# Two joints of a float32 encoder trunk rebuilt: halves of the last unit, raw residual turned, 1/rms applied late

## The reference

```python
def rms_norm(x, g):
    y = xf * lax.rsqrt(jnp.mean(xf * xf, axis=-1, keepdims=True) + NORM_EPS)
    return (y * g.astype(jnp.float32)).astype(x.dtype)
...
x = x + jnp.concatenate([oa, ob], axis=-1) @ w_out_e[i]          # first output projection
x = x + (silu(h @ w_gate) * (h @ w_up)) @ w_down                 # dense layer, h = rms_norm(x, ln_ffn_e)
h = rms_norm(x, ln_mix_o[j])
qc, kc, vc = jnp.split(h @ na_w_qkv[j], 3, axis=-1)              # neighbourhood attention
x = x + neighborhood_attention(qc, kc, vc, na_rpb[j]) @ na_w_out[j]
x = x + moe_swiglu(rms_norm(x, ln_ffn_o[j]), ...)                # top-2-of-8 experts
return rms_norm(x, ln_final)
```

## Time and profile before

| what | us |
| --- | --- |
| median of three runs | 1477.28 |
| lowest and highest of them | 1470.55, 1479.37 |
| the profiled execution, its own time | 1470.76 |
| its span | 1469.0 |
| PE, DVE, ACT busy in the span | 1432.2, 1116.0, 958.9 |

### The profile page before, as it was taken

One profiled execution on the slowest core, in us unless ns is written; L12 is line 12 of the kernel. 1 busy time (PEld: TensorE's weight loads), 2 busy tenths in 40 slices (PEclk: granted clock), 3 DMA queues, 4 the chain that ended last, 5 costly groups with the idle time before them and its releaser, 6 DMA issues.

```text
span 1469.0 us, 20948 instructions
## 1 busy us (share of the span) xinstructions
PE 1432.2 (97%) x7757; PEld 1224.7 (83%) x7757; DVE 1116.0 (76%) x843; ACT 958.9 (65%) x866; POOL 113.7 (8%) x99
## 2 busy tenths in 40 slices
PE   8989999999999999999999999999999999999996
PEld 7887999998987788888888888888888888888885
DVE  4574544456464698988888888898888888888886
ACT  6473443445354577777777777777777777777774
POOL 4340000000000110020001002002002000000100
PEclk9999999999999999999999999999999999999998
DMA  9422855554512499999999999999999999999992
GB/s 338 177 87 86 210 197 173 198 172 160 190 52 80 163 370 376 367 359 394 395 357 395 390 357 384 395 373 367 394 378 366 394 380 354 394 393 362 392 396 106
DMA packets 205850, 435.94 MB, mean 297 GB/s; under 512 B 8192, under 2 KB 53376, under 8 KB 205808
## 3 DMA queue, kind: packets, MB, share of 16 engines
q1 hardware_dynamic: 198176, 418.01, 78.2%
q0 software_dynamic: 3904, 14.42, 3.2%
q10 hardware_dynamic: 3728, 2.95, 1.0%
HBM read 428.02 MB, written 7.34 MB: 296 GB/s over the span
## 4 chain that ended last, share of the span: by engine, by line
PE 92%; DVE 5%; ACT 2%; issue 1%; DMA 0%; DVEq 0%; SPq 0%; ACTq 0%
PE banks L1274 29%; PE banks L1276 29%; PE banks L1275 29%; PE banks L1620 2%; PE banks L1467 1%; DVE w_lo L808 1%; DVE xn L821 1%; ACT arena L586 0%; PE banks L1586 0%; DVE arena L982 0%; PE banks L1289 0%; PE banks L1455 0%; PE banks L1396 0%; DMA xres<-in_x 0%; PE banks L1330 0%
## 5 line engine op out<-in xcount | busy, mean ns | idle before, releaser
L808 DVE TENSOR_TENSOR w_lo<-raw,w_hi 128x2048 fp32r<-128x2048 f32 (+1 forms) x396 | 904.1, 2291 | 221.3 <-ACT w_hi L453 220.4
L453 ACT CAST w_hi<-raw 128x2048 fp32r<-128x2048 f32 (+1 forms) x396 | 756.7, 1911 | 244.6 <-PE banks L1276 236.1
L1274 PE MATMUL banks<-w_hi,t_hi 128*128 128x512 f32 (+2 forms) x1088 | 416.4, 383 | 4.7 <-DVE w_lo L842 2.4
L1276 PE MATMUL banks<-w_lo,t_hi 128*128 128x512 f32 (+2 forms) x1088 | 410.9, 378 | 0.0
L1275 PE MATMUL banks<-w_hi,t_lo 128*128 128x512 f32 (+2 forms) x1088 | 410.5, 377 | 0.0
L1274 PEld LDWEIGHTS banks<-w_hi,t_hi 128*128 128x128 f32 x1088 | 205.6, 189 | 41.4 <-DVE w_lo L842 2.6
L1276 PEld LDWEIGHTS banks<-w_lo,t_hi 128*128 128x128 f32 x1088 | 205.5, 189 | 38.2
L1275 PEld LDWEIGHTS banks<-w_hi,t_lo 128*128 128x128 f32 x1088 | 205.7, 189 | 36.0 <-issue 0.2
L1274 PE MATMUL banks<-w_hi,h_hi 128*128 128x512 f32 x536 | 209.6, 391 | 0.7 <-DVE w_lo L808 0.7
L1276 PE MATMUL banks<-w_lo,h_hi 128*128 128x512 f32 x536 | 208.8, 390 | 0.0
L1275 PE MATMUL banks<-w_hi,h_lo 128*128 128x512 f32 x536 | 208.7, 389 | 0.0
(11 more groups left out here) (235 smaller groups left out, 937.1 us busy)
## 6 DMA issues: line engine op xcount, KB each, us to landing
raw<-in_moe_w_gate SPq DMA_DIRECT2D x112, 1024.0 KB, 7.8
raw<-in_moe_w_up SPq DMA_DIRECT2D x112, 1024.0 KB, 8.2
raw<-in_moe_w_down SPq DMA_DIRECT2D x112, 1024.0 KB, 8.1
raw<-in_na_w_qkv SPq DMA_DIRECT2D x12, 1024.0 KB, 5.1
raw<-in_ffn_w_gate SPq DMA_DIRECT2D x11, 1024.0 KB, 5.5
raw<-in_ffn_w_up SPq DMA_DIRECT2D x11, 1024.0 KB, 5.2
raw<-in_ffn_w_down SPq DMA_DIRECT2D x11, 1024.0 KB, 4.9
raw<-in_w_in_e SPq DMA_DIRECT2D x6, 1024.0 KB, 19.9
```

The source lines that it names most:

```text
L453: act.copy(w_hi[:, u.part, 0:n], raw[:, u.raw, 0:n]).then_inc(hi_done, 1)
L808: dve.tensor_tensor(w_lo[:, u.part, 0:n], raw[:, u.raw, 0:n], w_hi[:, u.part, 0:n].bitcast(F32), ALU.subtract).then_inc(lo_done, 1)
L1274: pe.matmul(out, a_hi, b_hi, start=start, stop=False)
L1276: return pe.matmul(out, a_hi, b_lo, start=False, stop=stop)
```

## The change

- The last unit of the first output projection and of the dense layer is computed by column halves (`rows_by_half`): all matmuls of columns 0 to 511 first, then those of columns 512 to 1023; the first half signals `half_mm`. DVE adds the residual in four 128 x 512 pieces (`residual_by_half`), the first two after the first half.
- `turn_x` turns the raw residual, half by half, in place of xn. `keep_busy` is gone at both joints. `turned_hi` and `turned_lo` split with the gain per partition (`gain_t` now holds four gains, the DMA of it is four times as large), 1/rms is computed afterwards (`row_stats`, `row_factors`).
- 1/rms is applied later: in the dense layer to the gate (a new DVE multiplication with `r_row` into `act_g`, silu then works in place) and to the output, as the factor of `residual_by_half`; in the neighbourhood layer to values (two ACT instructions with scale in place of one copy), to keys (a DVE multiplication into `k_tmp_c`, in xn, from which ACT and DVE split), and to the scores through `rq`. Two more `spread_rows`: after the first gate unit, and after the second unit of the neighbourhood projection.
- The gains of the last two norms are loaded at the start on POOL's queue; the loads of two others are gone, and with them two DMAs from ACT's queue.
- The second output projection and its joint stay as they were.

Lines with only "..." mark what is left out.

```diff
+BY_HALF = (U_OUT0,)
...
+        k_tmp_c = xn[:].rearrange("p t (i a s) -> p (t i) a s", i=2, a=2)
...
+            def turned_hi(q, n, bank):
+                for i in range(4):
+                    act.wait_ge(t_mm, 4 * q + i + 1)
+                    for k in (2 * i, 2 * i + 1):
+                        last = act.activation(t_hi[:, k, :], banks[:, bank + i, (k % 2) * SEQ:(k % 2 + 1) * SEQ],
+                                              ACT.Copy, scale=gain_t[:, n, k:k + 1])
+                    last.then_inc(t_hi_done, 1)
+            def row_stats(n):
+                for t in range(T):
+                    act.activation(xn[:, t, :], xres[:, t, :], ACT.Square,
+                                   accum_out=sums_sq[:, t:t + 1]).then_inc(ss_done, 1)
+                act.wait_ge(ms_done, 2 * n + 2)
+                act.activation(std[:], mean_sq[:], ACT.Sqrt).then_inc(std_done, 2)
...
-            norm_stats(1, ACT.Silu)
-            split_t_hi(2)
+            warm(ACT.Sqrt)
+            turned_hi(2, 1, 0)
+            row_stats(1)
+            warm(ACT.Silu)
             hi(Unit(U_FFN + 2))
-            act.wait_ge(xn_ready, 4)
-            act.dma_start(gains[:, 1, :], over_partitions(ln_ffn_o, D)).then_inc(gain_in[3], 16)
+            act.wait_ge(row_mm, 2)
+            act.copy(r_row[:], banks[:, 3, 0:SEQ]).then_inc(row_out, 1)
...
-                act.wait_ge(used, u.count())
-                act.activation(act_g[:], banks[:, 4 + 2 * jj, :], ACT.Silu).then_inc(silu_done, 1)
+                act.wait_ge(gate_scaled, j + 1)
+                act.activation(act_g[:], act_g[:], ACT.Silu).then_inc(silu_done, 1)
...
                 elif i < 8:
-                    last = act.copy(vc[:, :, 256 * (i - 4):256 * (i - 4) + 256], src)
+                    act.wait_ge(rstd_done, 6)
+                    for t in range(T):
+                        last = act.activation(vc[:, t, 256 * (i - 4):256 * (i - 4) + 256], src[:, t, :], ACT.Copy,
+                                              scale=rstd[:, t:t + 1])
                 else:
-                    last = act.copy(kc_t[0][:, 2 * (i - 8):2 * (i - 8) + 2, :], src)
+                    act.wait_ge(k_scaled, 2 + i - 7)
+                    last = act.copy(kc_t[0][:, 2 * (i - 8):2 * (i - 8) + 2, :], k_tmp_c[:, i - 8])
...
+            def turned_lo(q, n, bank):
+                for i in range(4):
+                    dve.wait_ge(t_hi_done, 4 * q + i + 1)
+                    for k in (2 * i, 2 * i + 1):
+                        last = dve.scalar_tensor_tensor(
+                            out=t_lo[:, k, :], in0=banks[:, bank + i, (k % 2) * SEQ:(k % 2 + 1) * SEQ],
+                            scalar=gain_t[:, n, k:k + 1], in1=t_hi[:, k, :].bitcast(F32),
+                            op0=ALU.mult, op1=ALU.subtract)
+                    last.then_inc(t_lo_done, 1)
+            def row_factors(n):
+                dve.wait_ge(ss_done, 2 * n + 2)
+                dve.tensor_scalar(mean_sq[:], sums_sq[:], 1.0 / D, EPS, ALU.mult, ALU.add).then_inc(ms_done, 2)
+                dve.wait_ge(std_done, 2 * n + 2)
+                dve.reciprocal(rstd[:], std[:]).then_inc(rstd_done, 2)
+                dve.wait_ge(rstd_done, 2 * n + 2)
+                dve.tensor_scalar(rq[:], rstd[:], HD ** -0.5, None, ALU.mult)
+                for t in range(T):
+                    last = dve.tensor_scalar(diag[:, t, :], ident, rstd[:, t:t + 1], None, ALU.mult)
+                last.then_inc(diag_ready, 1)
...
-                            in0=scores[:, cut].rearrange("p (r c) -> p r c", r=4), scalar=HD ** -0.5,
+                            in0=scores[:, cut].rearrange("p (r c) -> p r c", r=4), scalar=rq[:, t:t + 1],
...
+            def residual_by_half(n, bank, u, factor=None):
+                for c in range(2):
+                    if c == 0:
+                        dve.wait_ge(half_mm, n)
+                    else:
+                        dve.wait_ge(used, u + 1)
+                    for t in range(T):
+                        cols = xres[:, t, c * HALF:(c + 1) * HALF]
+                        out_half = banks[:, bank + 2 * t + c, :]
+                        if factor is None:
+                            dve.tensor_tensor(cols, cols, out_half, ALU.add).then_inc(x_tile, 1)
+                        else:
+                            dve.scalar_tensor_tensor(out=cols, in0=out_half, scalar=factor[:, t:t + 1], in1=cols,
+                                                     op0=ALU.mult, op1=ALU.add).then_inc(x_tile, 1)
...
-            residual(4, U_OUT0 + 3)
-            dve.wait_ge(x_tile, 2)
-            norm_apply(1, 1)
-            split_t_lo(2)
+            residual_by_half(1, 4, U_OUT0 + 3)
+            turned_lo(2, 1, 0)
+            row_factors(1)
             lo(Unit(U_FFN + 2))
-            def ffn_dve(j, jj):
+            def ffn_dve(u_g, u_u, j, jj):
+                dve.wait_ge(used, u_g.count())
+                both = lambda w: w.rearrange("p (k s) -> p k s", k=2)
+                dve.tensor_tensor(both(act_g), both(banks[:, 4 + 2 * jj, :]),
+                                  r_row[:].unsqueeze(1).broadcast_to([P, 2, SEQ]), ALU.mult).then_inc(gate_scaled, 1)
                 dve.wait_ge(silu_done, j + 1)
+                dve.wait_ge(used, u_u.count())
                 dve.tensor_tensor(hid[:], act_g[:], banks[:, 5 + 2 * jj, :], ALU.mult).then_inc(hid_done, 1)
...
                 elif i >= 8:
-                    c = slice(2 * (i - 8), 2 * (i - 8) + 2)
-                    rest(kc_t[1][:, c, :], kc_t[0][:, c, :], 4 + i % 4, 8 + i + 1)
+                    dve.wait_ge(used, U_QKV + i + 1)
+                    dve.wait_ge(row_out, 3)
+                    dve.tensor_tensor(k_tmp_c[:, i - 8], banks[:, 4 + i % 4, :].rearrange("p (a b) -> p a b", a=2),
+                                      r_row[:].unsqueeze(1).broadcast_to([P, 2, SEQ]), ALU.mult).then_inc(k_scaled, 1)
+            for i in range(4):
+                c = slice(2 * i, 2 * i + 2)
+                dve.wait_ge(proj_out, 16 + i + 1)
+                dve.tensor_tensor(kc_t[1][:, c, :], k_tmp_c[:, i], kc_t[0][:, c, :].bitcast(F32),
+                                  ALU.subtract).then_inc(qk_rest, 1)
...
+            def rows_by_half(u, bank, lhs_hi, lhs_lo):
+                pe.wait_ge(lo_done, u.count())
+                hi_w, lo_w = unit_parts(u, 2, D)
+                for c in range(2):
+                    cols = slice(c * HALF, (c + 1) * HALF)
+                    for i in range(2):
+                        for t in range(T):
+                            last = three(banks[:, bank + 2 * t + c, :], lhs_hi(i, t), lhs_lo(i, t),
+                                         hi_w[:, i, cols], lo_w[:, i, cols], False, i == 1)
+                    if c == 0:
+                        last.then_inc(half_mm, 1)
+                last.then_inc(used, 1)
+            def turn_x(n, bank):
+                for c in range(2):
+                    for t in range(T):
+                        pe.wait_ge(x_tile, 4 * (n - 1) + 2 * c + t + 1)
+                        for k in range(4):
+                            kk = 4 * c + k
+                            last = pe.transpose(banks[:, bank + kk // 2, (2 * (kk % 2) + t) * P:(2 * (kk % 2) + t + 1) * P],
+                                                xres[:, t, kk * P:(kk + 1) * P], ident)
+                            if t == T - 1 and k % 2 == 1:
+                                last.then_inc(t_mm, 1)
...
-            keep_busy(0, GAP)
-            transpose_xn(2, 2)
+            turn_x(1, 0)
...
                 columns(u_g, 4 + 2 * jj, 256, True, split).then_inc(used, 1)
+                if split is not None:
+                    spread_rows(2)
                 columns(u_u, 5 + 2 * jj, 256, True).then_inc(used, 1)
...
             pe.wait_ge(tab_b, 3)
+            pe.wait_ge(row_out, 2)
             for b in range(4):
                 clear(b)
...
-            ffn_down(Unit(U_FFN + 32), FFN_STEPS - 1, 0, True)
-            keep_busy(6, GAP)
-            transpose_xn(3, 4)
+            pe.wait_ge(h_hi_done, FFN_STEPS)
+            pe.wait_ge(h_lo_done, FFN_STEPS)
+            rows_by_half(Unit(U_FFN + 32), 0, lambda k, t: h_hi[:, 0, k * SEQ + t * P:k * SEQ + (t + 1) * P],
+                         lambda k, t: h_lo[:, 0, k * SEQ + t * P:k * SEQ + (t + 1) * P])
+            turn_x(2, 4)
...
+                if i == 1:
+                    spread_rows(3)
```

More of the change, by code:

```diff
@@ L158, in trunk @@
         gains = sb("gains", [P, 2, D])
-        gain_t = sb("gain_t", [P, KD])
+        gain_t = sb("gain_t", [P, 4, KD])
         r_row = sb("r_row", [P, SEQ])
@@ L662, in _ @@
                     hi(Unit(U_QKV + 3 + i))
+                if i == 1:
+                    act.wait_ge(row_mm, 3)
+                    act.copy(r_row[:], banks[:, 3, 0:SEQ]).then_inc(row_out, 1)
                 qkv_out(i)
@@ L1041, in _ @@
                         lo(Unit(U_FFN + 3 + 3 * jj + i, it))
[L1042 removed]
```

(20 more changed lines are left out.)

57 lines of the change are left out of this document (29 added, 28 removed).

## The result

| | before | changed |
| --- | --- | --- |
| median of five runs, us | 1474.3 | 1467.66 |
| lowest, highest | 1470.55, 1479.37 | 1463.61, 1468.37 |
| the profiled execution, span | 1469.0 | 1466.6 |
| its granted clock | 0.994 | 0.990 |

The ratio is 0.9949, with a 95% interval of 0.9933 to 0.9966: faster by 0.5%, which is 7.5 us on 1474.3. The forecast was -8.9 us, 0.6%, and "within 1%". (Two more runs of before had moved its median from 1477.28 to 1474.3.) The interval stands for 5.0 to 9.9 us, so it holds the forecast, and with -6.5 and -5.5 the prediction's rivals 1 and 2 too: the time alone can't choose between them. The two profiled executions are only 2.4 us apart, and a reader who compares just these two would say that three quarters of the gain are missing. The traces tell where they are.

A forecast was written before the change was run, and what follows sets the result against it. TensorE, 92% of the span, was taken as the bound. Joints -5.4 and -5.4, `spread_rows` +1.0, scores with keys +0.9 sum to -8.9 us: 1468.4 us from a median of 1477.28, range 1459 to 1474.

The forecast's parts named there:

- Rival 1: Both joints: pieces wait for the whole unit, so halving leads nowhere, 1.2 us later twice; -6.5, 1470.8 us; chance 0.11.
- Rival 2: Both joints: without fillers the clock falls, up to 1.7 us each, +3.4; so -5.5, 1471.8 us; chance 0.12.
- Joints: First output projection to dense layer, dense layer to neighbourhood projection: TensorE starts 5.6 us earlier, net -5.4 each.
- The pace of the following banks: After each joint: banks follow at 0.79 us, TensorE eats one in 0.72; three times 0.07, 0.2 lost.
- spread_rows: Added twice on TensorE, in the dense layer and neighbourhood projection: 0.48 us each, +1.0 in all.
- the keys: Neighbourhood projection: the last key scaling ends just as the first rest could start, +0.1 us.
- What moves behind: Squares, square root, reciprocal and diag beside the first unit's 48 matmuls: 0.9 us to spare, so no cost.
- Dense layer: 11 more DVE instructions for scaling the gate, 7.6 us, hidden: taken at 0, bounds -0.5 and +14.
- Start: DMA of the larger gain_t, waited for before the first split: taken at 0, bounds -0.1 and +0.5 us.
- Scores: Neighbourhood scores read their scalar from memory: +0.8 us, bounds 0 and 1.9.
- rival 3: Dense layer: the gate's scaling gets onto the path, 10 times 1.4 = 14 us; +5.5, 1482.8 us; chance 0.03.
- Rival 4: Clock falls at other places go away with the shift, 1.7 us each, scores cost nothing: -12, 1465 us; chance 0.12.

## Why the prediction was right

- **Joints.** Predicted 5.6 less 0.2 at each. Measured in the profile, from where the next instruction follows the unit's last matmul to the next product: 5.66 and 5.63 less. (From last matmul to product: 2.98 and 3.02, where the prediction had 2.6 to 3.0.) The chain was the predicted one, DVE's pieces at 137.52, right behind its `lo`, the first bank after six transposes, 0.87 from ACT's start to DVE's, TensorE 1.0 after that. Taking the fillers out is no gain of its own: before, TensorE still waited 0.17 for xn after the last of them, so it was the norm that held it.
- **The pace of the following banks** (0.2 lost) and **`spread_rows`** (0.48 each): the dense layer's first to last matmul took 0.55 more, the neighbourhood projection with the keys 0.6, against 0.5 + 0.2 and 0.5 + 0.2 + 0.1 of the sum. `spread_rows` itself took 0.45 (147.25 to 147.62, and 0.08 on the matmul behind it), so the pace cost about 0.1, half of what I had taken.
- **What moves behind** had its cover: the table, diag and the next unit's parts never kept TensorE. DVE's two instructions for diag end at 145.95 and TensorE asks at 147.25: 1.3 us to spare, 0.9 predicted.
- **Dense layer:** at 0, confirmed with three more multiplications per step. In the changed kernel's profile a silu ends at 216.70, and DVE's multiplication behind it starts at 217.04, released by TensorE's up unit: silu is out of the way, as predicted, by 0.3 us.
- **Start:** at 0. The first product comes at 9.37 to 9.84 us in the changed kernel and those made from it without fillers there, at 9.47 to 9.81 in the kernel before and its kin: the larger `gain_t` costs nothing that shows.
- **Scores:** the largest miss of a term. Taken at 0.8 between bounds of 0 and 1.9, measured 1.25. That is two thirds of DVE's 1.9 us, where I had taken under a half.
- **Sum without the clock:** -5.6 - 5.6 + 0.55 + 0.6 + 1.25 = -8.8, predicted -8.9. That the sum fits to 0.1 is in part luck: the scores cost 0.45 more than taken, the pace of the banks some 0.25 less, and the joints and `spread_rows` came out 0.15 better together. The ratio's 7.5 us and the 8.7 between the means (1475.5 of 25 runs, 1466.8 of 5; 8.2 with the five runs of before beside it) stand around it. What the profiled pair lacks (6.4) is the clock: the rows "-0.8", "+3.5" and what "+5.0" has over the scores' 1.25 sum to 6.4, and by the clock's column 6.8 us more of full speed were lost in that one execution. (The -0.8 is well within what executions differ by: in the ten profiles without a fall from 18 to 29 us the first output projection starts at 116.1 to 117.5.)
- **The forecast time** of 1468.4 against 1467.66 fits better than it deserves: it started from a median of 1477.28 of three runs, and 25 later runs have 1475.49, which would have given 1466.6.
- **Rival 2**, the clock at the joints: all nine kernels that turn the raw residual kept 1.00 at both joints in their profiles, 18 joints of 2.7 to 4.0 us without a filler. The clock falls elsewhere, and there its price is the rival's 1.7 us of full speed or more, up to 10.2. Ahead of three of the changed kernel's four falls TensorE stood still, for 1.95 us before 73.75, 1.37 before 441.20 and 1.17 before 498.09; ahead of the fourth, at 487, it ran matmuls of 8 columns. At the new joints it stands for 0.55 and 0.40 us. By the Trainium skill ("TensorE: Matmul & The Clock Gate", Part 1) an idle TensorE goes back to 1.2 GHz; the traces agree in part, since no fall came where the first two of these stands were filled, but the fall at 487 had no stand of that length ahead of it (0.72 us at most, before 481.93). Whether transposes count as activity (its Part 4) these runs don't tell apart.
- **Rival 1** fell with the halving undone, **rival 3** with the gate scaled four times. **Rival 4** had it that falls would go away with the shift; in the profiled execution there were more, and the mean clock of the runs did not move (0.9908, before 0.9913).

What stays open: whether the changed kernel falls more often than before at 442 to 454. Four of six unfilled kernels with the change showed a fall there, none of three filled; of the unfilled kernels with the old joints, one profile showed none and one (halving alone) a fall from 455 to 466, the same stage. The mean clocks speak for no difference.

## What to carry to other kernels

When a norm stands between two products, its 1/rms can leave the path whole: turn and split the raw values, and put the row factor on results that have slack. Halving the last unit pays most when what follows can take the halves one by one. And before a change of half a per cent is judged, put the granted clock of both traces side by side, stage by stage: landmarks at equal clock repeat here to some 0.02 us and gave each term to 0.1, while single executions of one kernel lie 9 us apart.

## What the runs showed that I had not expected

- A DVE instruction of 128 x 256 with its scalar from memory takes 0.475 us against 0.415 with a constant, in the same line of code (32 of each).
- Falls of the clock cost 1.7 us of full speed and more, up to 10.2 in one place (480 to 501 with fewer fillers in the routing), and the same program at a clock of 0.988 and of 0.994 is 8 us apart, without a change to it.
- The clock's column can read 1.00 at the start of an execution while the products go at half pace; the distances between starts tell.
- Fillers can cost what they save. Nine of them at the start made the first product 0.3 to 1.6 us later than in the profiles without; at half clock eight of them last 3.57 us in the routing, and with four in their place the mean was 3.6 us higher and the profile's clock stayed down into the experts.
